# Silu and gating of the seven-product chunks planned one step apart, behind the additions into the banks

## The reference, cut to what matters

```python
h = rmsnorm(x, ffn_norm_g[i])
hid = h @ w_ffn_in[i]              # 256 x 2048 @ 2048 x 11264
gate = hid[..., :FFN_HIDDEN]       # FFN_HIDDEN = 5632
up = hid[..., FFN_HIDDEN:]
x = x + (jax.nn.silu(gate) * up) @ w_ffn_out[i]
```

## Time and profile before

| what | value |
|---|---|
| median of 3 runs | 2416.97 us (2416.27 to 2420.19) |
| profiled execution, its own time | 2417.29 us |
| its span, first to last instruction | 2415.5 us |
| PE busy | 2399.9 us, 99% |
| DVE busy | 1725.7 us, 71% |
| ACT busy | 1341.7 us, 56% |
| POOL busy | 189.4 us, 8% |
| granted TensorE clock | 0.999 |
| DMA | 545.86 MB, 226 GB/s |

### The profile page before, as it was taken

How to read it: one execution, slowest core, us unless ns; L and a number is a source line. 1 busy time by engine, 2 the same in 40 slices (tenths; PEclk the granted TensorE clock), 3 DMA queues, 4 the chain that set the end, 5 groups by cost and what they waited for, 6 DMA issues and landing times.

```text
span 2415.5 us, 27959 instructions
## 1 busy us (share of the span) xinstructions
PE 2399.9 (99%) x10618; PEld 1983.9 (82%) x10618; DVE 1725.7 (71%) x2122; ACT 1341.7 (56%) x1641; POOL 189.4 (8%) x349
## 2 busy tenths in 40 slices
PE   9999999999999999999999999999999999999998
PEld 8888888888887787888888888888888888888887
DVE  7575555667778888669786865786577766778886
ACT  7555566445555555545455654545566666665554
POOL 0000000001000000000001010110111111110000
PEclk9999999999999999999999999999999999999999
DMA  8777665778766767776678787887788888886664
GB/s 275 224 220 231 199 189 180 221 233 252 225 209 207 228 209 221 228 217 212 198 229 274 239 241 213 256 248 235 234 246 246 243 243 240 241 241 216 215 205 158
DMA packets 155014, 545.86 MB, mean 226 GB/s; under 512 B 20096, under 2 KB 20608, under 8 KB 154624
## 3 DMA queue, kind: packets, MB, share of 16 engines
q1 hardware_dynamic: 131120, 470.91, 62.5%
q0 software_dynamic: 23184, 72.37, 11.4%
q10 hardware_dynamic: 576, 0.79, 0.1%
HBM read 505.72 MB, written 38.27 MB: 225 GB/s over the span
## 4 chain that ended last, share of the span: by engine, by line
PE 87%; DVE 6%; ACT 3%; DMA 2%; issue 1%; SPq 0%; ACTq 0%; DVEq 0%
PE ps L1842 86%; DVE wl L1278 2%; ACT wh L926 1%; DMA raw<-in_w_ffn_in 1%; DVE wl L1315 1%; ACT wh L950 1%; ACT tmp L966 1%; DVE tmp L1306 1%; DMA raw<-in_w_down 0%; DVE tmp L1309 0%; DVE tmp L1311 0%; DVE Y L1393 0%; DVE tmp L1353 0%; ACT act_hi L1089 0%; DVE tmp L1351 0%
## 5 line engine op out<-in xcount | busy, mean ns | idle before, releaser
L1278 DVE TENSOR_TENSOR wl<-raw,wh 128x1024 fp32r<-128x1024 f32 x794 | 965.9, 1221 | 622.9 <-ACT wh L926 621.4
L926 ACT CAST wh<-raw 128x1024 fp32r<-128x1024 f32 x794 | 828.6, 1049 | 752.1 <-PE ps L1842 732.0
L1842 PE MATMUL ps<-wh,x4g_hi 128*128 128x512 f32 x704 | 273.9, 389 | 0.0
L1842 PE MATMUL ps<-wl,x4g_hi 128*128 128x512 f32 x704 | 273.9, 389 | 0.0
L1842 PE MATMUL ps<-wh,x4g_lo 128*128 128x512 f32 x704 | 273.9, 389 | 0.0
L1842 PE MATMUL ps<-wh,x1g_hi 128*128 128x512 f32 x592 | 230.3, 389 | 0.0
L1842 PE MATMUL ps<-wl,x1g_hi 128*128 128x512 f32 x592 | 230.3, 389 | 0.0
L1842 PE MATMUL ps<-wh,x1g_lo 128*128 128x512 f32 x592 | 230.3, 389 | 0.0
L1842 PE MATMUL ps<-wh,h_hi 128*128 128x512 f32 x576 | 225.2, 393 | 0.6 <-ACT wh L931 0.6
L1842 PE MATMUL ps<-wh,h_lo 128*128 128x512 f32 x576 | 223.8, 391 | 0.0
L1842 PE MATMUL ps<-wl,h_hi 128*128 128x512 f32 x576 | 223.5, 390 | 0.0
(11 more groups left out here) (378 smaller groups left out, 3955.2 us busy)
## 6 DMA issues: line engine op xcount, KB each, us to landing
raw<-in_w_in SPq DMA_DIRECT2D x196, 512.0 KB, 4.4
raw<-in_w_ffn_in SPq DMA_DIRECT2D x176, 512.0 KB, 4.3
raw<-in_w_up SPq DMA_DIRECT2D x176, 512.0 KB, 4.7
raw<-in_w_ffn_out SPq DMA_DIRECT2D x88, 512.0 KB, 4.1
raw<-in_w_down SPq DMA_DIRECT2D x88, 512.0 KB, 4.2
rows<-Y POOLq DMA_DIRECT2D x67, 512.0 KB, 5.7
Z<-rows POOLq DMA_DIRECT2D x268, 128.0 KB, 4.9
raw<-in_w_o SPq DMA_DIRECT2D x32, 512.0 KB, 4.5
```

The costliest lines, as they stand in the source:

```text
L926: e.copy(wh[:, i % RING, :], raw[:, slot, :]).then_inc(rounded, 1)
L1278: e.tensor_tensor(wl[:, r, :], raw[:, i % RAW, :], wh[:, r, :].bitcast(F32), ALU.subtract).then_inc(remainder, 1)
L1842: return e.matmul(dst, weights, x, start=start, stop=stop, skip_group_check=True)
```

## The change

The silu of a chunk of a pair is planned one step behind its addition into the banks, and the gating one step behind the silu. The turn and all that follows for the rows of a pair keep their distance from the second chunk's gating, and so move by two steps. The silu phase waits for `shared_last` as well, as the part of `tmp` that it writes is read there. Chunks 0, 1 and 18 to 21 are not touched.

```diff
@@ plan_gated(n), after(s, chunk)
                 chunk.drained = [("silu", n), ("gated", n)]
                 if n // 2 in GATED_PAIRS:
                     do("shared_bank", n)
-                do("silu", n)
-                do("gated", n)
+                    later(s + 1, lambda: do("silu", n))
+                    later(s + 2, lambda: do("gated", n))
+                    s += 2
+                else:
+                    do("silu", n)
+                    do("gated", n)
 
                 def leave():
                     rows_of["act1", n // 2] = turn(s + 1, ST, ("gated", n))
@@ scalar(e), phase silu
                     e.wait_ge(*gated_at(n))
+                    if n // 2 in GATED_PAIRS:
+                        e.wait_ge(*at("shared_last", "gated", n // 2))
                     e.activation(ST[:, 0, sl], banks(chunk)[0][:, 0:T], ACT.Silu, scale=RT[:, 0:1]).then_inc(done[name], 1)
```

## The result

The changed kernel takes 2411.39 us (median of 7 runs, 2409.14 to 2411.6) against 2417.03 us before (7 runs beside it): a ratio of 0.9973, 95% interval 0.9964 to 0.9983. That is 5.6 us faster, clear of noise and inside the range; the forecast was 8.9. The profiled execution has a span of 2409.7 us, 5.8 less than before. The range holds the measured time only because it left room for a rival: the case that was given 0.63 was 2407 to 2409.5.

A forecast was written before the change was run, and what follows sets the result against it. PE's matmul stream was taken as the bound, losing time where it waits for DVE and ACT at units of pairs. Terms -8.2 and -0.97 gave -9.2, taken as -8.9: 2408.1 us from 2416.97, range 2406.5 to 2412.2.

The forecast's parts named there:

- the case that was given 0.63: Main forecast: losses at all first units and nearly all second units of the pairs go; 2407 to 2409.5 us.
- The ceiling: Side-by-side pairs: a better order can return at most 9.2 us by PE's starts, 4.8 by idle time.
- The first unit: First unit of pairs 2 to 8: DVE arrives 2.13 us earlier, both PE waits go seven times, -8.2 us.
- The price of the split: DVE before the drain: moving the split costs 1.20 us and gets 1.04 back from a hole, 0.16 net.
- of the wait, nothing: Silu's added wait on shared_last costs nothing, as silu already waits for shared_bank, which stands behind it in DVE's queue.
- The second unit: Second unit of a pair: its forms come in time, so three small PE losses go too, -0.97 us.
- landings past 6.9: Sign of being wrong: the second unit's sums starting more than 6.9 us behind the first unit's base_lo.
- the threshold of 6.88: Second unit: forms are in time for fetch landings up to 6.88 us, computed with base_lo 1.77 ahead.
- the second unit takes the loss: Rival, chance 0.14: transfer out nearer the fetches, landings 1 us longer, second units lose; gain 6 to 7, 2411 us.
- The holes: Rival, chance 0.12: DVE's silu holes stay in part, some 0.6 kept of each 1.17; gain 4, 2413 us.

The follow-up runs named there:

- The version with the bring held: Changed kernel, POOL's four transfers back of the rows of pairs 1 to 7 held until the next pair's second-unit granules landed; 2407.6 us, ratio 0.9961.
- only gated later: Against the changed kernel with those transfers back held: silu again in the step of the bank addition, gating one step later; 2423.06 us.
- the leave beside the fetches: Changed kernel, transfer out of the rows of pairs 1 to 7 held until base_lo of the next pair's first unit, transfers back after it; 2407.72 us.

## Why the prediction was right, and where it was off

**The ceiling.** 9.2 us by PE's starts, not 4.8 by its idle time. The version with the bring held gains 9.4 and has no gap left in the stage. Idle time alone would have missed half.

The Trainium skill (Perfetto Trace Analysis, section Identifying the Most-Contended Engine) calls matmul busy time a poor measure of how near a kernel is to its roofline, since matmuls are pipelined. The trace agrees that they are: they last 0.39 us and start 0.23 apart. How near this kernel is to a roofline no run here shows.

**The first unit.** Right, in mechanism and size. DVE was to come with base_lo 1.77 and forms_lo 1.13 ahead of PE; it came 1.57 and 0.93 ahead (it had come 0.36 late for gated_lo). All seven waits went. That the cast behind silu is the hinge was argued; the run with only gated later shows it, with the holes where the layout put them and the time forecast at 2422 measured at 2423.06. The price of the split, 0.16, and of the wait, nothing, were measured as stated.

**The second unit.** This is the step that failed. The prediction's own sign of being wrong, landings past 6.9, came in four of seven pairs. I took the landings of the kernel before, 5.36 to 6.33 us, as those of the kernel after, and the threshold of 6.88 as never reached; so the term was -0.97. It measured +3.5 - 0.97 = +2.5, with landings of 6.59 to 8.23. The threshold was a little too high: with the lead as measured, 1.57 and not 1.77, the same sum gives 6.68, and the pairs bear that out (6.59 costs nothing, 6.80 costs 0.19). So even by the prediction's sum two pairs under 6.88 lost time.

The rival "the second unit takes the loss" foresaw the place, and with a landing 1 us longer gave 2411, which is the time measured; I had given it 0.14. That its number came out is in part luck, as the transfer that it blamed was the wrong one. It named the leave, moved nearer to the fetches, and in the changed kernel the leave has landed before they are issued. I noted that the leave would go out with less beside it, and did not follow this on: it would land 3 us sooner and so set the bring on the very moment of the two fetches. The runs show that the leave beside the fetches, issued just behind them, lengthens the landings by 0.6 to 0.9 us and costs PE nothing, and that the bring beside them costs all of the 3.5.

The rule of the Trainium skill (DMA: Bandwidth & Descriptors, section Issuing engines are not separate DMA queues), that all issuing engines share the DMA engines, fits both: the trace agrees that transfers of POOL's queue slow SP's fetches (landings of 6.59 to 8.23 us beside the bring, 4.87 to 5.13 without). It gives the size of neither.

**Nothing else moved.** The holes did not come back (that rival is out), and the other stages gave and took nothing: the stage's own sum, -5.7, is the whole difference.

## What to carry to other kernels

Where two engines pass one tile back and forth, look for the operation of the long stream that stands in the queue behind the one that waits; here a step of delay for the waiting one (silu) brought DVE 1.9 us forward against PE, of which PE could use 1.2 at each first unit, and delaying only the other side of the exchange (gated) made it worse. When an engine comes earlier, follow each transfer that it releases up to the next one released by its landing, and set both against the tightest fetch: a chain of transfers that nobody is waiting for can be held back by one wait, and here that was worth 3.8 us. And price a PE stall by start-to-start distances.

## What the runs showed of the hardware that was not expected

What 512 KB cost two fetches of 512 KB beside them went from under 1 us to over 3, by their kind or by their moment; the runs do not part the two. The second of the fetches landed 4.3 to 4.6 us behind its issue with nothing of POOL's beside it (bring held), 5.2 to 5.3 beside a transfer out of 128 partitions to HBM issued 0.2 us behind it, and 6.1 to 7.7 beside the four transfers back, to 32 partitions each, of which the first was issued 0.2 to 0.6 us ahead of it.

A wait costs PE more than the idle time shown. With 0.61 us of idle time at a first unit 1.17 were lost. In the earlier trace rows the start at 782.59 comes 0.74 us behind the one at 781.85, where 0.23 is the steady distance: 0.51 lost, 0.35 of it shown as idle and 0.16 the overlap of two matmuls (0.39 long, 0.23 apart) that the wait takes away. The matmuls right behind a wait start up to 0.11 late as well (785.51 behind 785.17).
